# Nine pairs in the ring of gathered rows, eight diagonals of weights

## What is computed

```
q = (xb @ w_query).reshape(tb, PEER_HEADS, 2, PEER_KEY_DIM // 2)
s = jnp.einsum('thpd,pnd->thpn', q, sub_keys)
top_s, top_i = lax.top_k(s, k)
...
best_s, best_j = lax.top_k(cand_s.reshape(tb, PEER_HEADS, k * k), k)
idx = jnp.take_along_axis(cand_i.reshape(tb, PEER_HEADS, k * k), best_j, axis=-1)
gate = jax.nn.softmax(best_s, axis=-1)
u = expert_u[idx]
act = jax.nn.gelu(jnp.einsum('thkd,td->thk', u, xb))
w = gate * act
return jnp.einsum('thk,thkd->td', w, expert_v[idx])
```

## Time and profile before

| | us |
|---|---|
| median of 3 runs | 1789.01 |
| lowest and highest run | 1788.41, 1792.72 |
| span of the profiled execution | 1789.1 |
| busy: TensorE matmul | 1474.1 (82%) |
| busy: VectorE | 1149.3 (64%) |
| busy: GpSimd | 545.9 (31%) |
| busy: ScalarE | 437.1 (24%) |
| first gather issued, last one issued | 255.8, 1759.0 |

### The profile page before, as it was taken

The page is one execution under the profiler, slowest core; times in us unless marked ns, Lnnn a source line. Parts: engine busy times, 40 slices in busy tenths (PEclk is TensorE's granted clock), DMA queues, the critical chain, the costliest instruction groups (busy, mean ns, idle before and its releaser), DMA issues.

```text
span 1789.1 us, 14676 instructions
## 1 busy us (share of the span) xinstructions
PE 1474.1 (82%) x4075; PEld 683.3 (38%) x4075; DVE 1149.3 (64%) x2944; ACT 437.1 (24%) x1161; POOL 545.9 (31%) x583
## 2 busy tenths in 40 slices
PE   7999988877988777979878877977887977877875
PEld 3456535333533333434333523433333532333332
DVE  3344245666677768675786767676786777767764
ACT  1023212222134222331222222332221222222221
POOL 1011022233333333223333333333233333433331
PEclk9999998998999998989888998989888999999999
DMA  5120225998999999989999999999999999999995
GB/s 185 57 94 1 94 94 240 387 403 336 358 420 423 412 415 374 382 356 405 386 410 399 407 425 364 419 392 422 369 387 414 377 391 426 427 419 427 419 426 245
DMA packets 108095, 616.71 MB, mean 345 GB/s; under 512 B 10827, under 2 KB 12363, under 8 KB 40438
## 3 DMA queue, kind: packets, MB, share of 16 engines
q0 software_dynamic: 76032, 553.68, 75.2%
q1 hardware_dynamic: 31990, 62.17, 9.5%
HBM read 614.77 MB, written 1.05 MB: 344 GB/s over the span
## 4 chain that ended last, share of the span: by engine, by line
PE 45%; DMA 31%; DVE 14%; issue 6%; ACT 2%; POOL 1%; SPq 0%; DVEq 0%; POOLq 0%
DMA arena<-peer_uv,idx 29%; PE bank L852 22%; PE bank L644 13%; DVE arena L1554 5%; PE bank L826 2%; PE bank L753 2%; PE bank L747 2%; ACT arena L1156 1%; POOL arena L590 1%; PE bank L707 1%; PE bank L718 1%; DMA wring<-gla_w_in 1%; PE bank L801 1%; DVE wgt L1575 1%; PE bank L633 1%
## 5 line engine op out<-in xcount | busy, mean ns | idle before, releaser
L852 PE MATMUL bank<-arena 128*128 128x512 f32 x1944 | 959.0, 641 | 274.4 <-ACT arena L1156 250.3
L1554 DVE CUSTOM_DVE_ANT_0 arena<-arena,bank 128x1024 f32<-128x1024 f32 x528 | 640.7, 1219 | 423.4 <-DMA arena<-peer_uv,idx 419.9
L590 POOL DMA_INDIRECT arena<-peer_uv,idx x528 | 516.4, 978 | 1009.0 <-PE bank L852 946.5
L852 PEld LDWEIGHTS bank<-arena 128*128 128x128 f32 x1944 | 380.1, 204 | 810.3 <-issue 782.1
L1156 ACT ACTIVATE arena<-con,wgt 128x128 f32<-128x128 f32 x486 | 170.8, 394 | 795.6 <-DVE wgt L1575 775.9
L644 PE MATMUL bank<-wring,hT 128*128 128x512 f32 (+5 forms) x604 | 259.9, 585 | 1.0 <-DMA wring<-gla_w_in 0.7
L644 PEld LDWEIGHTS bank<-wring,hT 128*128 128x128 f32 (+1 forms) x604 | 109.0, 182 | 147.3 <-issue 142.1
L1145 ACT ACTIVATE gl<-dots 128x2 f32<-128x2 f32 x264 | 53.6, 203 | 288.9 <-DVE dots L1554 287.9
L1575 DVE SCALAR_TENSOR_TENSOR wgt<-gate_e,z,gl 128x2 f32<-128x2 f32 x264 | 57.6, 218 | 12.2 <-ACT gl L1145 5.8
L1560 DVE SCALAR_TENSOR_TENSOR h<-arena,wgt,h 128x1024 f32<-128x1024 f32 x42 | 53.9, 1284 | 1.6 <-DVE wgt L1575 0.2
L1145 ACT ACT_TABLE_LOAD x39 | 50.0, 1283 | 0.7
(11 more groups left out here) (157 smaller groups left out, 923.8 us busy)
## 6 DMA issues: line engine op xcount, KB each, us to landing
wring<-gla_w_in SPq DMA_DIRECT2D x12, 2048.0 KB
arena<-peer_uv,idx POOLq DMA_INDIRECT x528
wring<-gla_w_out SPq DMA_DIRECT2D x4, 2048.0 KB
wring<-peer_w_query SPq DMA_DIRECT2D x4, 2048.0 KB
wring<-attn_w_in SPq DMA_DIRECT2D x2, 2048.0 KB
wring<-attn_w_out SPq DMA_DIRECT2D x2, 2048.0 KB
gws<-peer_w_query SPq DMA_DIRECT2D x2, 2048.0 KB, 10.2
wring<-attn_w_in SPq DMA_DIRECT2D x1, 1664.0 KB
```

Of the source, the lines that this page charges most:

```text
L590: nc.gpsimd.indirect_dma_start(out=uvrow[:, n % RING, :], out_offset=None, in_=io["peer_uv"].rearrange("l e d -> (l e) d"), in_offset=bass ...
L852: last = nc.tensor.matmul(yacc[:, 512 * i:512 * i + 512], wdiag[:, k, :], rows_of(g, k, 1)[:, 512 * i:512 * i + 512], start=first, stop=la ...
L1554: v.tensor_tensor_reduce(out=rows, in0=rows, in1=xnow, scale=1.0, scalar=0.0, op0=ALU.mult, op1=ALU.add, accum_out=dots[:, g % 2, k:k + 1] ...
```

## The change

`RING` becomes 9, so that the ring holds nine pairs, slot n modulo 9, and gather n waits for pair n - 9. The diagonals get `DIAGS` = 8 places in place of 16: pair k of a tile has place k modulo 8, and ScalarE writes it when TensorE has used the last diagonal that lay there, as a rule that of pair n - 8. `arena` grows by 2 x 1024 words a partition for the slot and shrinks by 8 x 128 for the diagonals, together 1024 words (4 KB) more. The loops of tile 0 that were written with `RING` keep their counts (8 and 3). Nothing else changes: the same 528 gathers, the same arithmetic.

```
-RING = 8
+RING = 9
+DIAGS = 8
...
-        arena = sb("arena", [P, RING * 2 * D + TOPK * P])
+        arena = sb("arena", [P, RING * 2 * D + DIAGS * P])
...
-        wdiag = part(arena, RING * 2 * D, TOPK, P)
+        wdiag = part(arena, RING * 2 * D, DIAGS, P)
...
-                        last = nc.tensor.matmul(yacc[:, 512 * i:512 * i + 512], wdiag[:, k, :],
+                        last = nc.tensor.matmul(yacc[:, 512 * i:512 * i + 512], wdiag[:, k % DIAGS, :],
...
-                    before = [t for t in range(g) if k in by_tensor(t)][-1:]
+                    before = [n for n in range((TOPK * g + k) % DIAGS, TOPK * g + k, DIAGS) if n % TOPK in by_tensor(n // TOPK)][-1:]
                     if before:
-                        wait_second_used(act, before[0], k)
-                    nc.scalar.activation(wdiag[:, k, :], ident if g else const("place"), ACT.Copy,
+                        wait_second_used(act, before[0] // TOPK, before[0] % TOPK)
+                    nc.scalar.activation(wdiag[:, k % DIAGS, :], ident if g else const("place"), ACT.Copy,
                                          scale=wgt[:, g % 2, k:k + 1]).then_inc(diag_ready, 1)
...
-            for k in range(RING):
+            for k in range(TOPK // 2):
                 dot(0, k)
...
-            for j in range(RING // GROUP - 1):
+            for j in range(GROUPS // 2 - 1):
                 weigh(0, j)
-            for k in range(RING, TOPK):
+            for k in range(TOPK // 2, TOPK):
                 dot(0, k)
```

More of the change, by code:

```diff
@@ L253, in build @@
         rt = take(4 * NB * HALF * ROPE)
-        assert at <= RING * 2 * D + TOPK * P, at
+        assert at <= RING * 2 * D + DIAGS * P, at
         wq0 = part(gws, 0, 2, KC, 512)
```

## The result

| | before | after |
|---|---|---|
| median, us | 1790.9 (1788.4 to 1795.3, 4 runs) | 1743.8 (1737.7 to 1748.2, 4 runs) |
| span of the profiled execution | 1789.1 | 1746.4 |
| first gather issued | 255.78 | 258.34 |

The ratio is 0.9731 (95% interval 0.9707 to 0.9754): the change takes 47 us off.

What follows compares the result with a forecast made beforehand. The prediction took the DMA engines' gathers as the bound, 2.47 us a pair, with idle time in short stalls. Six stalls at 2.47 (14.8) plus shorter ones (6.9) gave 21.7 us: 1789.1 - 21.7, forecast 1767 us, range 1752 to 1784.

Steps and rivals of the forecast that it cites:

- The term for the stalls: Listed DMA stalls: each gives back the smaller of its idle time and one pair, 2.47 us; together 21.7 us.
- At 689: Stall from 689 to 693 us, 2.2 us idle: gain counted as 0, given back at the weight load at 736 us.
- the two double stalls: Stalls at 454 and 467, and at 794 and 803 us: each couple counts once, 2.47 us together.
- is all that a deeper ring can touch: Earlier stages' idle DMA time by share (30.5 or 41.7 us) plus the first stall's 18.6 us limits any gain.
- Once for each mixer: Rival: in each GLA mixer only the last stall's lead counts, 2.47 us each; sum 14.6, 1774.5 us; chance 0.20.
- The latency of a pair is the limit: Rival: each stage gains up to 9/8 in rate until idle time is gone; 44.2 us, 1745 us; chance 0.06.
- No effect: Rival: DMA engines are the limit in truth, or stalls move instead of shrinking; 1789 us; chance 0.09.
- The rule that I weighed: Skill's limit of about 358 GB/s a core for HBM transfers: gain would be 0; prediction let the trace decide.
- Weights late: Rival: weight loads beside gathers each take one gather longer, TensorE waits; 1817 us if all 20; chance 0.04 for slower.
- The weight load at 736 us: Load of the first half of GLA value weights: one more queued gather delays its end by up to 2.47 us.
- The diagonals: Eight places for sixteen add a wait for pair n - 8 on ScalarE; below 1 us a stall, taken as 0.
- Rate in the last stage: Stage at full DMA share, 1500 to 1760 us: same 424 GB/s and 2.47 us a pair after the change.

Runs made afterwards that it cites:

- r8_d8: The changed kernel with RING put back to 8, so only the eight diagonal places remain of the change: 1788.8 us, ratio 1.000.
- r9_wait8: The changed kernel with nine slots and eight diagonals, but gather n waits for pair n - 8 as before: 1792.8 us, ratio 1.001.
- r9_again: The changed kernel run once more, unaltered, as the measure for the others on the same chip: 1742.3 us, ratio 0.972.

## Why the prediction was wrong

**The bound and the mechanism were right.** The gathers set the pace, stalls empty their queue, and one slot more puts one gather ahead. That the depth alone does it is shown by r8_d8 and r9_wait8 (nothing) and by the two kernels that use it in part (29.6 + 18.7).

**The term for the stalls was right in size**: 21.7 forecast, 20.4 measured. The first one, 2.47 forecast, gave 2.6; that at 415, 2.47 forecast, gave 3.1; those at 337, 1189 and 1303 went as forecast. At 1084, 1410 and 1432 they went too, at 885 (870 of after) nothing changed, where I had 1.5. At 689, where I had 0, 0.8 came. That the sum is so near is partly luck: the two double stalls gave 1.3 (454 and 467) and 1.6 (794 and 803), where I had 2.47 each, and three single ones gave more than the 2.47 that I took as the most a stall can give (415: 3.1, 1084: 2.8, 1265: 2.9).

**The step that failed** is the sentence that the idle time by share "is all that a deeper ring can touch", with its bracket that the rest of the lower rate is the weight loads. The rows of before had the numbers that spoke against it: rates of 390 to 397 GB/s at a share of 0.97, which I put down to weights without working it out. The gathers alone moved 553.68 MB in 75.2% of 1789.1 = 1345.4 us of packet time, 412 GB/s, where the last stage had 424 / 1.01 = 420. At 420 they need 1318 us, so 27 us were in the gathers' packets and not in the weights. The gain of the profiled execution, 42.7 us, is made up as follows: the gathers begin 2.56 us later (258.34 for 255.78, ahead of all that changed), so 45.3 us were gained from there on. 17 us of it are packet time (14.6 gathers, 2.3 weights), the term that was missing. The remaining 28.4 us are idle time, 20.4 in the listed stalls and some 8 outside them. Forecast 21.7, measured 20.4 + 8 + 17. The packet records, added up from the first packet of a gather to the last, say nearly the same: the time went from 1512.2 to 1466.7 us, the packets' part from 1463.8 to 1445.0 (18.8 less) and the idle part from 48.4 to 21.7 (26.7 less, of which 6 lie off the list). The other traces repeat it: 1462.6 and 1464.5 us of packets with 46.8 us idle in r8_d8 and r9_wait8, 1444.1 with 21 in r9_again. The series at fixed depth show the mechanism of the gathers' 15, that a thin queue looks busy, and the table by number of gathers out accounts for them. The weights' 2 us have no such account.

**Why it reaches so far beyond the stalls.** In before, 32% of the gathers' packets start with one or two gathers out, in after 20%. With seven slots the last stage runs at 391 GB/s, 2.68 us a pair: 7 x 2.68 = 18.8 us is about what a pair takes around the ring (transfer, two landings' wait, dot, gelu, weight, diagonal, mixing, next issue), or a little more, since at times that stage too is bound by the DMA engines. Eight slots at 2.46 us make 19.7 us. By this estimate (from the stage's rate alone; no view shows the whole way of a pair) the ring of before had about one microsecond to spare on average, and any work put in between thinned the queue, without a stall that the DMA share would show. I took the ring for deep enough outside the stalls because the last stage was at 424 GB/s; I should have worked out by how much it was.

**The rivals.** *Once for each mixer* (0.20): refuted, 29.6 us in the mixers' tiles. *The latency of a pair is the limit* (0.06, 1745 us): it has the measured time, and its picture (slots over cycle time) is the nearer one; but its sum assumed that all idle time goes, and of the first stall alone 16.0 us are left. It got its size from too much idle time and no packet time. Its chance was too low, and the range should have taken it in. *No effect* (0.09): refuted. The rule that I weighed did not hold here: the one core of this kernel gathers at 427 GB/s for whole slices. The Trainium skill, DMA: Bandwidth & Descriptors, section Bandwidth, has about 358 GB/s as a core's share with both cores of the memory domain streaming, a condition that the prediction left out; this kernel uses one. *Weights late* (0.04): refuted, next point.

**The weight load at 736 us.** I had TensorE's wait grow from 0.69 to 2 or 3 us and gave the stall at 689 no gain for that. It fell:

```profile
722.71 15.72 DMA wring<-gla_w_in
```

```profile
738.47 7.13 PE L645 MATMUL bank<-wring,hT 128*128 128x512 f32 x16 [0.38 <-DMA wring<-gla_w_in]
```

15.72 us from issue to use for 16.03, and 0.38 us of wait for 0.69. One more gather in the queue did not delay the load; why is open, as the gathers' places around it have shifted too.

**The diagonals.** Taken as 0, and 0 it is: r8_d8 measures nothing, and ScalarE's idle time ahead of L1157 is all for VectorE's weights (738.2 of 738.2), none for TensorE.

**Rate in the last stage.** Forecast unchanged. It is 427 GB/s in the slices of after and 422 for 420 over the whole stage, so that even there 2 us were to be had.

## What to carry to other kernels

For a stream that should be bound by DMA, compare bytes over time with the best stretch of the same trace, after taking out other traffic by its own cost; a busy share near 1 doesn't prove that the queue is full. Work out slots x transfer time against the time that a slot takes to come round. Here the two were within 5% by the estimate above, and a slot more, or a slot given back one step earlier (a weighing moved ahead by one dot, without any memory), was worth about twice the stalls that one could count. How far this holds at other margins wasn't measured; the ninth slot gave less than half of what the eighth had given.

## What the runs showed of the hardware

- Gathers of 128 rows of 8 KB: 179, 347, 419, 427 GB/s with one, two, three, four out at a time. The DMA engines' share was 0.52, 0.96, 1.01 and 1.01: at two, the share is 0.96 and the rate is 19% off. One run of that kernel was made.
- One such gather alone took 5.86 us from one to the next, issue included. The Trainium skill, DMA: Bandwidth & Descriptors, section "Anatomy of one DMA", gives 2.0 us and bytes over 436 GB/s; by that page's figures the estimate for 1.049 MB is 4.4 us. The measured value is larger by 1.5 us, of which GpSimd's instruction (0.94 us) may be a part.
- A packet of 8 KB took 309 ns with four or more gathers out. Into an empty queue, the first sixteen packets of a gather took 775 ns in the mean.
- The whole kernel with seven, eight and nine pairs in use: 1898, 1792 and 1742 us.
